# Feed-forward of a two-layer decoder on one core: the variance product and the token operands later, the second pair's transfer in front of the last stores, the last normalization summed in steps and in halves

## The reference, cut to what matters

```python
def _layer_norm(x, g, b):
    xc = xf - jnp.mean(xf, -1, keepdims=True)
    var = jnp.mean(xc * xc, -1, keepdims=True)
    return xc * lax.rsqrt(var + LN_EPS) * g + b

def _post_block(x, mix, w1, w3, w2, g1, b1, g2, b2):
    x = _layer_norm(ALPHA * x + mix, g1, b1)
    ff = (jax.nn.silu(x @ w1) * (x @ w3)) @ w2
    return _layer_norm(ALPHA * x + ff, g2, b2)
```

## Time and profile before

| | us |
|---|---|
| time, median of 3 runs | 3162.65 |
| lowest, highest | 3157.42, 3162.95 |
| profiled execution, its own time | 3146.89 |
| span of the profiled execution | 3145.1 |
| PE busy | 2831.1 (90%) |
| DVE busy | 1935.2 (62%) |
| ACT busy | 1270.1 (40%) |

### The profile page before, as it was taken

How to read it: one execution, slowest core, us unless ns; L and a number is a source line. 1 busy time by engine, 2 the same in 40 slices (tenths; PEclk the granted TensorE clock), 3 DMA queues, 4 the chain that set the end, 5 groups by cost and what they waited for, 6 DMA issues and landing times. The chain is left out here.

```text
span 3145.1 us, 54502 instructions
## 1 busy us (share of the span) xinstructions
PE 2831.1 (90%) x21507; PEld 2558.9 (81%) x21507; DVE 1935.2 (62%) x3821; ACT 1270.1 (40%) x2386; POOL 322.4 (10%) x281
## 2 busy tenths in 40 slices
PE   7999799987989999999997875758899999999996
PEld 7999466546889999999997863735499999999996
DVE  7885388746467655556456338978368555565455
ACT  5554177632435433344112215836336333343113
POOL 0000200004100000000000542834100000000000
PEclk9999999995789999999998986889899999999998
DMA  5554310023121222224220410410122222233211
GB/s 206 195 194 170 94 55 1 1 69 118 55 71 61 75 82 82 82 91 155 96 69 1 136 72 28 126 58 4 53 66 78 75 72 82 79 122 133 92 59 56
DMA packets 101579, 268.42 MB, mean 85 GB/s; under 512 B 15016, under 2 KB 45896, under 8 KB 91460
## 3 DMA queue, kind: packets, MB, share of 16 engines
q1 hardware_dynamic: 97908, 252.37, 23.4%
q0 software_dynamic: 1936, 9.38, 1.1%
q10 hardware_dynamic: 1488, 3.24, 0.3%
HBM read 210.15 MB, written 59.15 MB: 86 GB/s over the span
## 5 line engine op out<-in xcount | busy, mean ns | idle before, releaser
L1077 PE MATMUL f_acc<-f_x,f_w 128*128 128x264 f32 x2488 | 707.9, 285 | 7.5 <-DVE f_gated L1445 5.3
L1079 PE MATMUL f_acc<-f_x,f_w 128*128 128x264 f32 x2488 | 709.4, 285 | 0.0
L1078 PE MATMUL f_acc<-f_x,f_w 128*128 128x264 f32 x2488 | 705.4, 284 | 0.0
L1077 PEld LDWEIGHTS f_acc<-f_x,f_w 128*128 128x128 f32 x2488 | 470.7, 189 | 10.1 <-issue 9.2
L1078 PEld LDWEIGHTS f_acc<-f_x,f_w 128*128 128x128 f32 x2488 | 470.7, 189 | 0.2
L1079 PEld LDWEIGHTS f_acc<-f_x,f_w 128*128 128x128 f32 x2488 | 469.5, 189 | 0.0
L176 PE MATMUL f_acc<-f_h,f_w 128*128 128x352 f32 (+2 forms) x1056 | 345.5, 327 | 12.2 <-DVE xT_sb L1481 8.6
L177 PE MATMUL f_acc<-f_h,f_w 128*128 128x352 f32 (+2 forms) x1056 | 340.9, 323 | 0.0
L178 PE MATMUL f_acc<-f_h,f_w 128*128 128x352 f32 (+2 forms) x1056 | 340.4, 322 | 0.0
L1483 DVE TENSOR_TENSOR xT_sb<-xT_sb,f_acc 128x352 f32<-128x352 f32 (+2 forms) x208 | 108.7, 523 | 220.1 <-PE f_acc L178 220.1
L1319 DVE TENSOR_TENSOR f_w<-f_raw,f_w 128x512 fp32r<-128x512 f32 x208 | 142.9, 688 | 133.4 <-ACT f_w L1151 133.1
(11 more groups left out here) (527 smaller groups left out, 6324.2 us busy)
## 6 DMA issues: line engine op xcount, KB each, us to landing
f_raw<-w SPq DMA_DIRECT2D x52, 1024.0 KB, 4.9
pe_raw<-w_in_e SPq DMA_DIRECT2D x54, 512.0 KB, 4.4
f_hidden<-f_gated SPq DMA_DIRECT2D x88, 264.0 KB, 2.0
f_h_raw<-f_hidden SPq DMA_DIRECT2D x22, 1056.0 KB, 5.0
f_w_raw<-w SPq DMA_DIRECT2D x22, 1024.0 KB, 5.0
pe<-pe_y SPq DMA_DIRECT2D x54, 264.0 KB, 2.7
odd_oT<-w_in_o SPq DMA_DIRECT2D x18, 512.0 KB, 3.9
po<-po_y SPq DMA_DIRECT2D x8, 528.0 KB, 2.9
```

Source lines behind the costliest of these rows:

```text
L1077: pe.matmul(to, wh, xh, start=begins and t == 0, stop=False, skip_group_check=True)
L1078: pe.matmul(to, wh, xl, start=False, stop=False, skip_group_check=True)
L1079: mm = pe.matmul(to, wl, xh, start=False, stop=ends and t == KQ - 1, skip_group_check=True)
```

## The change

In `project_and_feed`, so twice in the kernel:

- DVE makes the low part of operand `B12` before the three additions of quarter 3, no longer behind them.
- `variance` of quarter 3 stands behind product 12, no longer behind product 9; `deviation` at n = 13 (was 9), `affine` at 16 (was 11), `invert` and `scale` at 13 (were at 10).
- The second half's token operands are prepared later, and in the order 7 to 13.
- `load_hidden(1)` stands in SP's queue in front of the stores of the last visit, no longer behind them.
- The first output of each group and pass waits tile by tile for its operands, no longer for all pairs of the group at its start. `low_h` and `low_w2` of the odd pairs stand one or two `add`s later.
- `variance` of parts 0 and 1 stands behind output 5 of the pass, no longer behind output 4.
- Last normalization: the sum over the tiles is made in steps between the last `add`s (`sum_more`), centring, squaring and the sum of squares in two halves, and of the 8 last affine steps 3 are done by DVE.

```diff
-    x_order = [0, 3, 5, B12, 1, 4, 2, 6, 8, 7, 9, 10, 11, 13, 12, B12 + 1]
+    x_order = [0, 3, 5, B12, 1, 4, 2, 6, 7, 8, 9, 10, 11, 12, 13, B12 + 1]
...
-    X_SUM = ((5, 1), (6, 4), (8, 2), (9, 6), (17, 8), (19, 11), (21, 9), (22, 13))
-    X_ROUND = ((7, 1), (10, 4), (11, 2), (13, 6), (19, 8), (20, 7), (24, 9), (25, 10), (26, 11), (28, 13), (32, 12), (TAIL + 2, B12 + 1))
-    X_REST = ((11, 1), (13, 4), (14, 2), (15, 6), (24, 8), (25, 7), (27, 9), (28, 10), (29, 11), (31, 13), (34, 12), (TAIL + 4, B12 + 1))
+    X_SUM = ((5, 1), (6, 4), (8, 2), (9, 6), (20, 8), (21, 11), (23, 9), (24, 13))
+    X_ROUND = ((7, 1), (10, 4), (11, 2), (14, 6), (22, 7), (23, 8), (26, 9), (29, 10), (33, 11), (35, 12), (37, 13), (TAIL + 2, B12 + 1))
+    X_REST = ((10, 1), (12, 4), (15, 2), (17, 6), (25, 7), (26, 8), (28, 9), (33, 10), (36, 11), (38, 12), (40, 13), (TAIL + 4, B12 + 1))
...
+    ON_ACT = 5
...
+                    if v == V - 1:
+                        load_hidden(1, units_of(FT - 1)[-1])
                     for u in units_of(v):
                         store(u)
-                load_hidden(1, units_of(FT - 1)[-1])
                 load2(1)
...
-                    if n == 9:
+                    if n == 12:
                         variance(QUARTERS - 1)
...
+                    for t in range(2 * len(pairs)):
+                        i, f = pairs[t // 2], t % 2
+                        if begins:
+                            pe.wait_ge(h_split, 2 * i + f + 1)
+                            pe.wait_ge(w2_split, 2 * i + f + 1)
...
-                        if c and m == 4:
+                        if c and m == 5:
                             variance(QUARTERS + c - 1)
...
-                    for kt in range(KT):
+                    for kt in range(KT if j < LAST_LN else ON_ACT):
...
-                    if n == 9:
+                    if n == 13:
                         deviation(3)
-                    if n == 11:
+                    if n == 16:
                         affine(3)
...
+                rest_x(B12)
                 sum_up(3)
-                rest_x(B12)
...
-                    if n == 10:
+                    if n == 13:
                         invert(3)
                         scale(3)
...
+                def sum_more(m):
+                    xs, sq = x(LAST_LN), squares(LAST_LN)
+                    total = 4 * LAST_LN
+                    if m == 5:
+                        dve.wait_ge(added, pass_at(3) + 4)
+                        dve.tensor_tensor(out=sq[:, 0:2], in0=xs[:, 0:2], in1=xs[:, 2:4], op=ALU.add).then_inc(added_up, 1)
+                        dve.wait_ge(added_up, total + 1)
+                        dve.tensor_tensor(out=sq[:, 0], in0=sq[:, 0], in1=sq[:, 1], op=ALU.add).then_inc(added_up, 1)
+                    dve.wait_ge(added, pass_at(3) + m)
+                    dve.wait_ge(added_up, total + m - 3)
+                    if m < KT:
+                        dve.tensor_tensor(out=sq[:, 0], in0=sq[:, 0], in1=xs[:, m - 1], op=ALU.add).then_inc(added_up, 1)
+                    else:
+                        dve.tensor_tensor(out=statistic(LAST_LN), in0=sq[:, 0], in1=xs[:, KT - 1], op=ALU.add).then_inc(summed, 1)
...
                         add(a * outs + i, m, CH, cols(c), first=a == 0)
-                        if i in (1, 3):
-                            low_h(2 * a + 1, i // 2)
-                        if i in (6, 8):
-                            low_w2(2 * a + 1, i // 2 - 3)
+                        if i in (2, 4):
+                            low_h(2 * a + 1, i // 2 - 1)
+                        if i in (8, 10):
+                            low_w2(2 * a + 1, i // 2 - 4)
...
                     invert(j)
                     scale(j)
                     for m in range(5, KT):
+                        if last:
+                            sum_more(m)
                         add(n + m, m, PARTS[c], part(c))
                 j = LAST_LN
-                sum_up(j)
-                centre(j)
-                sum_squares(j)
+                sum_more(KT)
+                for half in range(2):
+                    centre_half(half)
+                square_sums()
                 invert(j)
...
+                dve.wait_ge(scaled, j + 2)
+                for kt in range(ON_ACT, KT):
+                    xk = k.xT[:, kt, of(j)]
+                    dve.tensor_scalar(out=xk, in0=xk, scalar1=k.lnp[:, row + 1, 0, kt:kt + 1], scalar2=k.lnp[:, row + 1, 1, kt:kt + 1],
+                                      op0=ALU.mult, op1=ALU.add).then_inc(done, 1)
```

More of the change, by code:

```diff
@@ L1082, in _, with second @@
                         mean(QUARTERS - 1)
-                    if n == 9:
+                    if n == 12:
                         variance(QUARTERS - 1)
-                def second(n, m, columns, where, pairs):
+                def second(n, m, columns, where, pairs, begins):
                     if n == 2:
@@ L1090, in second @@
                         pe.wait_ge(added, n - 3)
[L1091 to L1094, removed]
+                    for t in range(2 * len(pairs)):
[3 more added lines that the diff above has]
+                            pe.wait_ge(w2_split, 2 * i + f + 1)
+                        mm = multiply_tile(pe, acc[:, B_BANK[n % 4], 0:columns],
+                                           lambda _: (W2[slot(i)][:, 0, f, m], W2[slot(i)][:, 1, f, m]),
+                                           lambda _: (H[slot(i)][:, 0, f, where], H[slot(i)][:, 1, f, where]), t, 2 * len(pairs))
+                    mm.then_inc(down, 1)
                 for a, pairs in enumerate(GROUPS):
[L1097 to L1098 removed]
                     for i in range(outs):
                         m, c = divmod(i, NCH)
[L1101 removed]
+                        second(a * outs + i, m, CH, cols(c), pairs, begins=i == 0)
                 for t, (c, pairs) in enumerate(passes):
[L1103 to L1104 removed]
                     for m in range(KT):
[L1106 removed]
+                        second(pass_at(t) + m, m, PARTS[c], part(c), pairs, begins=m == 0)
                         if c and m == 1:
                             mean(QUARTERS + c - 1)
[L1109 removed]
+                        if c and m == 5:
                             variance(QUARTERS + c - 1)
@@ L1253, in _ @@
                         high_w2(i, a)
-                for j in range(QUARTERS, LAST_LN + 1):
+                for j in range(QUARTERS, LAST_LN):
                     square(j)
@@ L1257, in _ @@
                     affine(j)
+                for half in range(2):
+                    kts = slice(half * KT // 2, (half + 1) * KT // 2)
+                    act.wait_ge(centred, LAST_LN + half + 1)
+                    if half == 0:
+                        act.wait_ge(summed, LAST_LN + 1)
+                    act.activation(squares(LAST_LN)[:, kts], x(LAST_LN)[:, kts], ACT.Square).then_inc(squared, 1)
+                deviation(LAST_LN)
+                affine(LAST_LN)
             @block_.vector
@@ L1475, in _, with centre_half, square_sums @@
                         low_w2(0, 1)
+                def sum_more(m):
[12 more added lines that the diff above has]
+                        dve.tensor_tensor(out=statistic(LAST_LN), in0=sq[:, 0], in1=xs[:, KT - 1], op=ALU.add).then_inc(summed, 1)
+                def centre_half(half):
+                    kts = slice(half * KT // 2, (half + 1) * KT // 2)
+                    dve.wait_ge(mean_of, LAST_LN + 1)
+                    dve.tensor_tensor(out=x(LAST_LN)[:, kts], in0=x(LAST_LN)[:, kts], in1=wide(mean_bank(LAST_LN), KT // 2),
+                                      op=ALU.subtract).then_inc(centred, 1)
+                def square_sums():
+                    sq, total = squares(LAST_LN), 4 * LAST_LN + 5
+                    dve.wait_ge(squared, LAST_LN + 1)
+                    dve.tensor_tensor(out=sq[:, 0:2], in0=sq[:, 0:2], in1=sq[:, 2:4], op=ALU.add).then_inc(added_up, 1)
+                    dve.wait_ge(squared, LAST_LN + 2)
+                    dve.tensor_tensor(out=sq[:, 4:6], in0=sq[:, 4:6], in1=sq[:, 6:8], op=ALU.add).then_inc(added_up, 1)
+                    dve.wait_ge(added_up, total + 2)
+                    dve.tensor_tensor(out=sq[:, 0:2], in0=sq[:, 0:2], in1=sq[:, 4:6], op=ALU.add).then_inc(added_up, 1)
+                    dve.wait_ge(added_up, total + 3)
+                    dve.tensor_tensor(out=statistic(LAST_LN), in0=sq[:, 0], in1=sq[:, 1], op=ALU.add).then_inc(squares_up, 1)
                 def add(n, m, columns, where, first=False):
@@ L1506, in _ @@
                 for c in range(1, NCH):
-                    j, n = QUARTERS + c - 1, pass_at(c + 1)
+                    j, n, last = QUARTERS + c - 1, pass_at(c + 1), c == NCH - 1
                     sum_up(j)
```

1 line of the change is left out of this document (added).

## The result

| | before | after |
|---|---|---|
| first timing, median (lowest to highest) | 3161.06 us (3157.42 to 3162.95, 4 runs) | 3121.85 us (3119.59 to 3126.18, 4 runs) |
| profiled execution, its own time | 3146.89 us | 3119.59 us |
| its span | 3145.1 us | 3117.8 us |

A forecast was written before the change was run, and what follows sets the result against it. PE, busy 90% of the span, bounds the kernel, so only its idle time and clock can gain. Terms 10.2 + 11.0 + 2.9 + 4.4 = 28.5 us take the median 3162.65 to 3134 us, range 3125 to 3149.

The forecast's parts named there:

- on the median 3162.65 - 28.5 = 3134: Whole kernel: the 28.5 us gain taken off the median of the runs before, giving 3134 us, 0.9% less.
- Quarter 3's mean: Part 2: PE idles 3.7 us at `mean`, then 2.0 us of low clock, and 0.3 us at product 18.
- rival C: Part 2: no low clock behind quarter 3's `mean`, 2.0 us less a call, 3130 us; chance 0.07.
- Variance and product 33: Part 2: idle 3.78 us at `variance` and 2.68 at product 33 go, with 2.35 and 1.5 of low clock.
- Rival B: Part 2: product 33 still waits, 1.4 us idle and 1.5 of clock back each call, 3140 us; chance 0.14.
- Part 3: Begin of part 3: earlier `load_hidden(1)` gains 6.5 us in f1, 4.5 in f0, 11.0 together, with 0.3 a call allowed.
- Rival A: Part 3: transfer still holds PE, 2 us idle a call and 1.5 of low clock, 3140 us; chance 0.13.
- the 1.5 us of low clock that I put beside each wait: Begin of part 3: low clock behind the 5.33 us wait costs 1.5 us in f1, the same taken for f0.
- The pass: Pass of pairs 9 and 10: waiting tile by tile leaves 0.35 us of 1.78, gaining 1.4 a call, 2.9 us.
- Last normalization: End of each call: gain 1.9 us in f1, 2.5 in f0; stepwise sum 0.75 us later, `mean` idle over 5 us.
- Slower (D): Part 2: plain products from 4 on stay at the low clock; to product 33, 3200 us; chance 0.03.
- each idle place of this size is followed by the low level: Part 2: every idle place of 2.67 us or more was followed by the low clock; 2.0 us added behind `mean`.

The follow-up runs named there:

- e1: The kernel before, unchanged, timed and profiled again; ratio 0.9998, median 3155.0 us.
- e16: e8 unaltered, a second time, against the kernel before; median 3114.97 us, ratio 0.9883.
- e5: The changed kernel, unaltered, timed anew against the kernel before; median 3123.67 us, ratio 0.9904.
- e15: The changed kernel, unaltered, a third time against the kernel before; median 3122.22 us, ratio 0.9903.
- e7: The changed kernel with `variance` of parts 0 and 1 behind output 4 again; median 3116.12 us, ratio 0.9878 of before.
- e11: The changed kernel with `load_hidden(1)` behind the last stores again; median 3126.02 us, ratio 0.9914 of before.
- e12: The changed kernel with the waits for all pairs at each group's start again; median 3129.44 us, ratio 0.9921 of before.
- e2: The kernel before with only the part 2 edits (quarter 3 and the token operands); ratio 0.9965.
- e4: The kernel before with only the last normalization's edits, `variance` behind output 5 included; ratio 0.9977.
- e8: The changed kernel with quarter 3's sums ahead of B12's low part and `variance` of parts 0 and 1 behind output 4 again; 3116.12 us, ratio 0.9878 of before.
- e6: The changed kernel with quarter 3's sums ahead of B12's low part again; median 3122.2 us, ratio 0.9893 of before.

## Why the prediction missed

**The step that failed** is "on the median 3162.65 - 28.5 = 3134". The sum of the steps was made against the profiled execution and came out there: 3118.4 us forecast, 3119.59 measured. But it was then put on the median of three runs, 15.8 us higher, as if that were the kernel's level. In the 50 runs of before that came with e1 to e16 its median is 3154.4 us (3146.61 to 3162.82), and only 13 of the 50 lie above 3157.42, the lowest of the four runs of the first occasion. The changed kernel is at 3121.85, 3123.67 and 3122.22 us on three occasions. 3154.4 - 28.5 = 3126 would have been 4 us high, and inside the range. Of the miss of 12 us, if 3154.4 is taken as the level, 8 came from the base, 2 from the steps (30.6 against 28.5), and 2 are the spread of four executions about 3154.4 - 30.6. For the base I had the means to know better: a profile 10.5 us below the lowest of three runs says that the kernel's executions spread by that much, and the range should have reached down by it too. That the forecast for the profiled execution came out within 1.2 us is in part luck: outside the two calls the pair of executions differed by 3.3 us the other way, which no step had foreseen, and inside them the gain was 2.1 us larger than forecast.

Why the kernel before was high on that one occasion, while the changed one was not, stays open. If the runs were independent draws from the 50, all four so high would be a matter of about 1 in 200, so the occasion itself probably differed; the later ones differ too, with medians of before of 3155.0 us on one chip, 3153.87 and 3153.52 on a second and 3149.86 on a third. A long execution of before goes with a low mean granted clock: with the 12 runs of e1 there are 62 with a clock on record, and the 4 at 0.928 have a median of 3158.5 us, the 5 at 0.934 one of 3149.9. Which of the two leads isn't shown, and no clock is on record for the four. The profiles show where executions of one kernel differ (ahead of f0, from 879.4 to 886.7 us, and between the calls, from 543.1 to 549.3 us over all profiles), not what sets it, and none was taken of one of those four runs.

**Step by step**, gains in us, each measured from the segments above:

| step | forecast f0, f1 | measured f0, f1 |
|---|---|---|
| start to part 3 (part 2) | 5.1, 5.1 | 5.4, 5.3 |
| part 3 to the passes | 4.5, 6.5 | 5.2, 7.0 |
| passes, last normalization | 3.9, 3.3 | 4.1, 3.5 |

- *Quarter 3's mean.* 3.7 us idle forecast, 3.53 or 3.54 measured in all twelve calls of the changed kernel (after, e5, e15) and of e7, e11 and e12. The clock was already at the lower level under the mean in seven of them, fell within 3 us behind its begin in three, and stayed at 1.00 up to product 18 in two. It changed the sum by 0.5 us only, because what is saved there is waited for at product 18: 24.62 or 24.63 us from the one to the other in the seven, 24.13 to 24.15 in the other five. I had 0.3 us at product 18 and 2.0 of clock. The sum of both was right and its parts were not independent, and rival C, which took the 2.0 off without a wait in its place, was wrong in that.
- *Variance and product 33.* No wait at either, in both calls, as forecast. Rival B did not come about. The terms of the walk to the sum of squares add up to 2405.9 from 2399.2, not to 2406.5; with 3 us of room the slip changes nothing.
- *Part 3.* No wait of over 0.25 us at its begin, in place of the 0.3 that I allowed, and 1.2 us more gain in the two calls than forecast. Rival A did not come about. It quoted a DMA share of 0.74 from a stretch of part 2; from the issue of the pair to its landing (2854.14 to 2861.36) the share in the kernel before was 0.95, so that the case for it was a little stronger than written. The size before is itself unsure: part 3 to the passes took 164.3 to 168.9 us in eight calls without these edits (before, e1, e2, e4), and 160.4 in every call with both of them. The ends are e4's f0, with 3.20 us idle and the clock at 1.00 behind it, and e1's f1, with 5.69 us and 0.50: the 1.5 us of low clock that I put beside each wait is not paid every time.
- *The pass.* 0.35 us forecast, 0.30 measured, and the variance's 0.60 and this 1.48 make 2.1 of the 2.4 us by which the passes are shorter; the other 0.3 I can't place.
- *Last normalization.* The mean's wait grew by 1.34 us; 0.75 for the steps and 0.60 for the end of the variance's wait make the same. I wrote "over 5 us" beside it, and it is 4.57, the size that my own terms give. VectorE's three affine steps took 1.11 us together, at the low end of my 1.1 to 1.4. The text has the later reciprocal as a loss next to the 0.60 us that `variance` behind output 5 saves, and e7 measures the two together: that edit costs 2.0 to 2.4 us a call, and about 3 by e8 against e6.
- *Slower (D).* The low clock behind the mean of f0 took 19 matmuls at 0.50 (row above); the 3 us behind them were granted 0.85, and the next 3 us 1.00. It lasted no longer than the 20 that I counted by more than a few.

## What to carry to other kernels

A sum of steps read from one profile forecasts the next profile; to forecast a median it needs the kernel's own level over many executions, and a profile that lies outside the few runs given says that this level is not known. Compare two kernels by marks around the changed stage before the whole span is compared: here the stage repeated within 1 us while the execution moved by 10.
A wait that goes away is a gain only up to the next thing that the same chain sets; the mean, product 18, product 22 and product 25 were one chain of ScalarE and VectorE, and only its order in both queues, looked at together, moved its end.

## What the runs showed of the hardware that was not expected

The same wait of 3.54 us, in the same place, was followed by the lower clock at different points, or not at all. In f0 of the first profile of the changed kernel the mean ran at 0.50, while f1 was granted 1.00 over the whole way to product 18:

```profile
2381.00:2405.10 24.10, 21.50 (x172) 1.00 0.17 55
```

In e5 it was f1 whose mean ran at the low clock, and in f0 the clock fell within 1 us behind the mean's begin. These are the mean's rows in e5 and the stretch behind the first:

```profile
995.13 0.76 PE L1020 MATMUL f_acc<-f_stat,mean_w_sb 128*128 128x264 f32 x2 [3.54 <-DVE f_stat L1295]
2389.84 1.25 PE L1020 MATMUL f_acc<-f_stat,mean_w_sb 128*128 128x264 f32 x2 [3.54 <-DVE f_stat L1295]
996.10:998.90 2.80, 2.80 (x15) 0.50 0.00 0
```

Of the fourteen calls with this wait (the twelve above and e2's) nine had the mean itself at the low clock (its two matmuls in 1.25 us), three had it just behind (0.71 to 0.76 us for the mean; f0 of e5 and e7, f1 of e11), and two not at all (f1 of the first profile and of e7, with 2.65 and 2.60 us of wait at product 18). Nor does the length of the wait decide it: TensorE was granted 1.00 behind 2.68 us at product 33 and behind 3.20 us where part 3 begins in e4's f0, and behind 2.16 and 2.86 us in e11, but 0.56 behind 1.83 us in e12's f0. So "each idle place of this size is followed by the low level", which I wrote of the kernel before, is not a rule. And a stretch of 90 us that the change does not touch was granted 0.89 in one execution and 0.85 in another of the same kernel, which came with 2.3 us more for the same matmuls.
